# Score products of a linear-attention branch issued as pairs of 64x64 products on two column tiles, and moved behind the weight tiles

## The chip, the cores and the metric

The kernel runs on one core of one Trainium2 chip. The metric is the device time of one execution in microseconds (us), and the number that counts is the median of several runs. TensorE (PE) does the matrix products, VectorE (DVE) and ScalarE (ACT) do elementwise work, GpSimd (POOL) prepares weights, SyncE (SP) issues the weight transfers. All five run their own instruction streams and wait for each other by semaphores.

## The reference, cut to what matters

The network is a trunk of two layers at 512 tokens and width 1024. The even layer mixes an HGRN2 branch (8 heads of 128) with an RWKV-7 branch (16 heads of 64). The change touches the scores of the HGRN2 branch, here for one head and one chunk:

```
G = jnp.cumsum(gc, axis=2)
diff = jnp.where(causal[:, :, None], G[:, :, :, None, :] - G[:, :, None, :, :], -jnp.inf)
attn = jnp.einsum('bhtk,bhsk,bhtsk->bhts', qc, kc, jnp.exp(diff))
o = jnp.einsum('bhts,bhsv->bhtv', attn, vc) + jnp.einsum('bhtk,bhkv->bhtv', qc * jnp.exp(G), state)
```

So `attn[t, s]` is a dot product over the 128 channels in which every channel is damped by the decay between s and t. The RWKV-7 branch is a recurrence over chunks of a state per head; its hops from chunk to chunk ("the chain" below) are what the score products are interleaved with.

## The kernel before

The even layer runs in nine rounds, `even_round(i)`, i = 0 to 8. Round i projects the input for head i (tiles 0 to 7, each `t(j)` made of two halves of 12 products of 512 columns, whose weights come in two units) and computes HGRN2 for head i, while RWKV-7 is computed for the pair of heads of round i - 1. Round 0 has no RWKV-7 part, round 8 has nothing else; rounds 1 to 7 have both, and rounds 2 to 7 are a hardware loop. The odd layer and the output projections follow and are not touched.

HGRN2 takes chunks of 128 tokens (CH = 4, L = 128) and builds the damping up in seven levels: level `lvl` covers the pairs of blocks of m = 2^lvl tokens, the later block being the queries and the earlier one the keys. VectorE and ScalarE rescale queries and keys from level to level (`level` L1375 on VectorE, `level_copies` L903 on ScalarE), TensorE multiplies them (`hg_level`, one 128x128 product per chunk into bank 2 or 3 of PSUM), and VectorE copies the pairs that belong to the level into `attn` with a mask (`masked`, L1398, by a predicated copy at L1361). Level 6 needs one 64x64 block per chunk alone and is already issued so. The diagonal (`hg_diagonal`) is an eighth set of products. Levels 0 to 5 and the diagonal have nonzero pairs only inside the two 64x64 blocks on the diagonal of a chunk.

The chain of RWKV-7 has three steps of TensorE per chunk: `chain_rhs` (rhs), `chain_u` (u) and `chain_out` (out). Between rhs and u, ScalarE copies the result out of PSUM (`chain`, L969), between u and out again, and between out of one chunk and rhs of the next VectorE updates the state (`state`, L1502; for chunks 1 and 2 these are the lines L1513 and L1516). TensorE's own order is written out by hand; its waits are in order, and so are those of every other engine. In VectorE's order, `state(r, 1)` stands behind the masked copies of levels 0 and 1, and `state(r, 2)` stands behind the masked copy of level 2, the rescaling of level 5 (L1394 to L1396) and the masked copy of level 3.

GpSimd splits every weight unit in two (L255 and L257) as soon as TensorE has finished the unit that held the same of four slots; `half_tile` waits for the split unit and, in its first half, for its PSUM bank.

Of the kernel before, what the change touches and what calls it, by code (L numbers as in the profile page):

```python
# [21 lines left out]
P = 128  # L22
KC = D // P
CH = 4
L = T // CH
# [62 lines left out]
def count(name, r, j=0):  # L88

    value = r * PER_ROUND[name] + j + 1  # L90
    assert not isinstance(value, int) or value > 0, (name, r, j)
    return value


def trunk(nc, xT, pT, wall, par_e, par_o, gains, w2a2, lru_w, masks, out):
    ctx = ExitStack()
    with ctx:
# [32 lines left out]
        psum = ctx.enter_context(nc.psum_tensor("psum", [P, 8, T], F32))  # L130
        bank = [psum[:, n, :] for n in range(8)]
        H0, H1, R0, R1, R2, R3 = bank[2:8]
# [15 lines left out]
        hq, hk, hf, hv, sig_a, sig_b, g_a = (place(T) for _ in range(7))  # L148
        qp = place(4 * T).rearrange("p (r t) -> p r t", r=4)
# [120 lines left out]
        def _(pe):  # L270
            def mm(o, lhsT, rhs, start=True, stop=True):
                return pe.matmul(o, lhsT, rhs, start=start, stop=stop, skip_group_check=True)  # L272
# [186 lines left out]
            def chain_u(r, c):  # L459

                pe.wait_ge(sem["rw_rhse"], count("rw_rhse", r, c))
                for e, rows in heads:
                    last = mm(R0[:, 64 + 64 * e:128 + 64 * e], inv[:, c, 2 + e, :], rhs_s[:, c % 2, rows])
                last.then_inc(sem["rw_u"], 1)
# [38 lines left out]
            def hg_level(r, lvl):  # L503

                o = bank[2 + lvl % 2]
                pe.wait_ge(sem["hg_lvl"], count("hg_lvl", r, lvl))
                if lvl:
                    pe.wait_ge(sem["hg_even"], count("hg_even", r, 2 * lvl - 1))
                if lvl == 0:
                    pe.wait_ge(sem["hg_vtok"], count("hg_vtok", r))  # L510
                elif lvl == 1:
                    if not (isinstance(r, int) and r == 0):
                        pe.wait_ge(sem["hg_n"], count("hg_n", r - 1))
                else:
                    pe.wait_ge(sem["hg_masked"], count("hg_masked", r, lvl - 2))
                keys = hk if lvl == 0 else kr[:, lvl % 4, :]
                for c in range(CH):
                    at = slice(c * L, (c + 1) * L)
                    if lvl < LEVELS - 1:
                        last = mm(o[:, at], keys[:, at], qp[:, lvl % 4, at])  # L520
                    else:
                        even, odd = slice(c * L, c * L + 64), slice(c * L + 64, (c + 1) * L)
                        last = mm(o[0:64, odd], keys[:, even], qp[:, lvl % 4, odd])
                last.then_inc(sem["hg_qk"], 1)

            def hg_diagonal(r):
                pe.wait_ge(sem["hg_masked"], count("hg_masked", r, 5))
                for c in range(CH):
                    last = mm(H1[:, c * L:(c + 1) * L], hk[:, c * L:(c + 1) * L], hq[:, c * L:(c + 1) * L])
                last.then_inc(sem["hg_qk"], 1)  # L530

            def hg_keys(r):
# [32 lines left out]
            def even_round(i, head=True, pair=True):  # L565

                r = i - 1
                first = isinstance(i, int) and i == 0

                def t(j, halves=(0, 1)):  # L570
                    if head or j == 0:
                        for half in halves:
                            half_tile(i, j, half, 0, "free", first and j < 2, 0 if first and j == 0 else None)

                def level(lvl):
                    if head:
                        hg_level(i, lvl)

                def embedding(m):
                    if not head:  # L580
                        if m == 0:
                            pe.wait_ge(sem["free0"], count("free0", EV_ROUNDS, 0))
                            pe.wait_ge(sem["free1"], count("free1", EV_ROUNDS - 1, 3))
                        else:
                            pe.wait_ge(sem["prj_evac"], count("prj_evac", 0, m - 1))
                        embed(0, m, U_PRJ0, (0, 1))

                t(0)
                if pair:
                    low_rank(r)  # L590
                t(1)
                if pair:
                    key_norm(r)
                    bonus(r)
                embedding(0)
                t(2)
                t(3)
                if pair:
                    transposes(r)
                    t(4, (0,))  # L600
                    for n in range(2 * CH):
                        product(r, n)
                        if n >= 3 and n % 2:
                            inverse_start(r, n // 2 - 1)
                    t(4, (1,))
                    inverse_start(r, 3)
                    for lvl in range(1, 7):
                        inverse(r, lvl)
                    chain_rhs(r, 0)
                    t(5, (0,))  # L610
                    chain_u(r, 0)
                    t(5, (1,))
                    chain_out(r, 0)
                else:
                    t(4)
                    t(5)
                embedding(1)
                if head:
                    hg_values(i)
                if pair:  # L620
                    chain_rhs(r, 1)
                level(0)
                if pair:
                    chain_u(r, 1)
                level(1)
                if pair:
                    chain_out(r, 1)
                embedding(2)
                t(6)
                if pair:  # L630
                    chain_rhs(r, 2)
                level(2)
                if pair:
                    chain_u(r, 2)
                level(3)
                if pair:
                    chain_out(r, 2)
                embedding(3)
                t(7)
                if pair:  # L640
                    chain_rhs(r, 3)
                level(4)
                if pair:
                    chain_u(r, 3)
                level(5)
                if pair:
                    chain_out(r, 3)
                level(6)
                if head:
                    hg_diagonal(i)  # L650
                    hg_keys(i)
                if pair:
                    head_mean(r)
                if head:
                    hg_changes(i)
                    hg_outputs(i)
                if pair:
                    head_var(r)
                if head:
                    hg_norm(i)  # L660
# [602 lines left out]
        def _(dve):  # L1263
# [48 lines left out]
                    ins.then_inc(sem["bias_set"], 1)  # L1312

            dve.memset(attn, 0.0)
            dve.memset(p_full, 0.0)
            dve.memset(shift[:, 0:1], 0.0)
            dve.memset(w2_slot[64:P, 0, :], 0.0)
# [589 lines left out]
```

## Time and profile before

| | us |
|---|---|
| median of 3 runs (range) | 1501.81 (1501.2 to 1503.7) |
| span of the profiled execution | 1501.0 |
| TensorE busy | 1391.1 |
| VectorE busy | 792.6 |
| ScalarE busy | 560.3 |
| GpSimd busy | 622.7 |

The profiled span runs from the first to the last instruction of the program and is 0.8 us under the median of the runs. An engine's busy time counts instructions in progress; waits, register and branch instructions do not count. TensorE's products overlap, and each product of 32-bit operands shows two entries (its two passes), each product of 512 columns with split operands shows one.

### The profile page before, as it was taken

How to read it: one execution, taken by the hardware profiler on the slowest of the kernel's cores; microseconds unless marked ns; L12 is line 12 of the kernel's file. 1: busy time of each engine (PE TensorE's matmuls, PEld its weight loads, DVE VectorE, ACT ScalarE, POOL GpSimd, SP SyncE). 2: the span in 40 equal slices, each digit the busy share in tenths (PEclk: the TensorE clock that was granted, in tenths of full speed). 3: DMA queues.
4: the chain of work that ended last, by engine and by line, in shares of the span. 5: the costliest groups of instructions: out<-in, count | busy, mean ns of one | idle time of the engine just before them, and what ended most of it. 6: DMA issues, size and time to landing. Idle time of an engine off the chain costs nothing. (4 is left out here: it accounts for less than half of the span.)

```text
span 1501.0 us, 24358 instructions
## 1 busy us (share of the span) xinstructions
PE 1391.1 (93%) x7722; PEld 1109.9 (74%) x7722; DVE 792.6 (53%) x1412; ACT 560.3 (37%) x1214; POOL 622.7 (41%) x584
## 2 busy tenths in 40 slices
PE   2999999999999999999999979899979999998995
PEld 1776877877878877868868857787757777776874
DVE  6546256365275374373373462207674747566457
ACT  3333344344244254244344353203242433335123
POOL 3643133242241350350251201577844636454872
PEclk9999999999999999999999989999979999999998
DMA  5211011011110120120120100333312212221331
GB/s 177 80 52 49 21 53 43 29 45 41 28 58 28 42 57 14 42 65 7 42 65 14 41 30 16 125 108 91 98 56 71 78 56 77 67 66 50 103 93 63
DMA packets 46687, 87.80 MB, mean 58 GB/s; under 512 B 5808, under 2 KB 6832, under 8 KB 46384
## 3 DMA queue, kind: packets, MB, share of 16 engines
q1 hardware_dynamic: 44352, 82.44, 18.5%
q10 hardware_dynamic: 2288, 4.72, 0.9%
q8 instruction: 31, 0.51, 0.1%
q14 instruction: 16, 0.13, 0.0%
HBM read 85.04 MB, written 2.10 MB: 58 GB/s over the span
## 5 line engine op out<-in xcount | busy, mean ns | idle before, releaser
L272 PE MATMUL psum<-h_split,w_hi 128*128 128x512 f32 x2320 | 754.5, 407 | 17.0 <-DVE h_split L1275 9.0
L255 POOL TENSOR_SCALAR w_hi<-w_raw 128x512 fp32r<-128x512 f32 x290 | 213.2, 735 | 828.1 <-PE psum L272 705.8
L272 PEld LDWEIGHTS psum<-h_split,w_hi 128*128 128x128 f32 x2320 | 438.9, 192 | 134.2 <-issue 37.8
L272 PE MATMUL psum<-mix 128*128 128x128 f32 (+4 forms) x3520 | 485.4, 292 | 19.2 <-ACT mix L831 7.0
L272 PE MATMUL psum<-h_split,w_lo 128*128 128x512 f32 x1160 | 458.8, 396 | 0.0
L272 PEld LDWEIGHTS psum<-mix 128*128 128x128 f32 (+1 forms) x3520 | 379.4, 176 | 89.5 <-issue 45.8
L257 POOL TENSOR_TENSOR w_lo<-w_raw,w_hi 128x512 fp32r<-128x512 f32 x290 | 410.5, 1416 | 24.2
L831 ACT ACTIVATE mix<-psum 128x256 f32<-128x256 f32 (+5 forms) x624 | 233.1, 391 | 459.8 <-PE psum L272 251.0
L272 PEld LDWEIGHTS psum<-h_split,w_lo 128*128 128x128 f32 x1160 | 222.1, 191 | 48.6
L1361 DVE COPY_PREDICATED mix<-mask,psum 128x128 f32<-128x128 uint8 (+2 forms) x312 | 135.6, 465 | 187.3 <-PE psum L272 184.3
L831 ACT ACTIVATE mix<-mix 128x512 f32<-128x512 f32 (+3 forms) x274 | 137.9, 538 | 158.9 <-DVE mix L1636 72.4
L831 ACT ACTIVATE mix<-psum,mix 128x512 f32<-128x512 f32 (+2 forms) x88 | 53.4, 631 | 170.1 <-PE psum L272 122.0
L272 PE MATMUL psum<-mix,fconst 128*128 128x512 f32 x90 | 51.1, 666 | 49.5 <-DVE mix L1295 38.7
L1271 DVE SCALAR_TENSOR_TENSOR mix<-psum,mix 128x512 f32<-128x512 f32 x40 | 29.5, 736 | 113.1 <-ACT mix L831 101.7
L1271 DVE SCALAR_TENSOR_TENSOR mix<-mix 128x512 f32<-128x512 f32 (+1 forms) x72 | 75.8, 1053 | 12.8 <-ACT mix L831 10.5
L272 PEld LDWEIGHTS psum<-mix,fconst 128*128 128x128 f32 x90 | 14.9, 200 | 65.1 <-issue 21.4
L419 PE MATMUL psum<-fconst,mix 128*128 128x128 f32 x320 | 62.1, 276 | 0.1
L1361 DVE COPY_PREDICATED psum<-mask,fconst 128x128 f32<-128x128 uint8 x32 | 14.6, 455 | 58.2 <-PE psum L272 58.2
L831 ACT ACT_TABLE_LOAD x23 | 29.5, 1283 | 41.5 <-PE psum L272 37.0
L1306 DVE TENSOR_TENSOR h_split<-y,h_split 128x512 fp32r<-128x512 f32 x28 | 25.2, 941 | 37.0 <-ACT h_split L831 37.0
L419 PEld LDWEIGHTS psum<-fconst,mix 128*128 128x128 f32 x320 | 39.3, 142 | 1.4 <-DVE mix L1361 0.3
L1275 DVE TENSOR_TENSOR h_split<-mix,h_split 128x512 fp32r<-128x512 f32 x32 | 34.7, 1085 | 10.7 <-ACT h_split L831 10.4
(118 smaller groups left out, 733.3 us busy)
## 6 DMA issues: line engine op xcount, KB each, us to landing
w_raw<-wall SPq DMA_DIRECT2D x290, 256.0 KB, 2.6
mix<-xT SPq DMA_DIRECT2D x4, 512.0 KB, 6.3
mix<-xT ACTq DMA_DIRECT2D x1, 2048.0 KB, 8.0
out<-mix SPq DMA_DIRECT2D x8, 256.0 KB, 2.1
mix<-mask_f SPq DMA_DIRECT2D x1, 1792.0 KB, 11.4
mix<-pT ACTq DMA_DIRECT2D x2, 512.0 KB, 3.5
mix<-lru_w ACTq DMA_DIRECT2D x4, 256.0 KB, 3.3
mix<-w2a ACTq DMA_DIRECT2D x16, 32.0 KB, 2.8
```

Of the source, the lines that this page charges most:

```text
L255: pool.tensor_scalar(w_hi[:, slot, :, :], w_raw[:, slot, :], 1.0, 0.0, ALU.mult, ALU.add).then_inc(sem["w_hi"], 1)
L257: pool.tensor_tensor(w_lo[:, slot, :, :], w_raw[:, slot, :], w_hi[:, slot, :, :].bitcast(F32).rearrange("p k n -> p (k n)"), ALU.subtract) ...
L272: return pe.matmul(o, lhsT, rhs, start=start, stop=stop, skip_group_check=True)
L419: last = pe.transpose(bank[2 + c % 2][:, e * P:(e + 1) * P], inv[:, c, e, :], ident)
L831: return act.activation(o, i, func, bias=bias, scale=scale, **kw)
L1271: return dve.scalar_tensor_tensor(out=o, in0=a, scalar=scalar, in1=b, op0=op0, op1=op1)
L1275: dve.tensor_tensor(h_split[:, KC + c, :], hn[:, c % 2, :], h_split[:, c, :].bitcast(F32), ALU.subtract).then_inc(sem["h_ready"], 1)
L1306: dve.tensor_tensor(h_split[:, KC + ring, :], y[:, rows[c], :], h_split[:, ring, :].bitcast(F32), ALU.subtract).then_inc(sem["y_split"], 1)
L1361: return dve.copy_predicated(dst, mask, src)
```

## The change

Each of the products of levels 0 to 5 and of the diagonal, 128x128 per chunk, becomes two 64x64 products per chunk: the even half of a chunk writes partitions 0 to 63 of PSUM (one column tile of the array, 64 columns wide), the odd half partitions 64 to 127 (the other column tile). The off-diagonal blocks of the two banks are not written any more, so they are set to zero once at the start. In TensorE's order, the tiles 6 and 7 move ahead: one half of tile 6 now stands between rhs and u of chunk 1 and one half behind u, and the levels 0 and 1 follow together, right ahead of out of chunk 1; the same is done with tile 7, chunk 2 and the levels 2 and 3. The levels 4 to 6, the diagonal and all orders of VectorE, ScalarE and GpSimd stay as they are, but for the one memset.

```
                 for c in range(CH):
-                    at = slice(c * L, (c + 1) * L)
+                    even, odd = slice(c * L, c * L + 64), slice(c * L + 64, (c + 1) * L)
                     if lvl < LEVELS - 1:
-                        last = mm(o[:, at], keys[:, at], qp[:, lvl % 4, at])
+                        mm(o[0:64, even], keys[:, even], qp[:, lvl % 4, even])
+                        last = mm(o[64:P, odd], keys[:, odd], qp[:, lvl % 4, odd])
                     else:
-                        even, odd = slice(c * L, c * L + 64), slice(c * L + 64, (c + 1) * L)
                         last = mm(o[0:64, odd], keys[:, even], qp[:, lvl % 4, odd])
...
                 for c in range(CH):
-                    last = mm(H1[:, c * L:(c + 1) * L], hk[:, c * L:(c + 1) * L], hq[:, c * L:(c + 1) * L])
+                    even, odd = slice(c * L, c * L + 64), slice(c * L + 64, (c + 1) * L)
+                    mm(H1[0:64, even], hk[:, even], hq[:, even])
+                    last = mm(H1[64:P, odd], hk[:, odd], hq[:, odd])
...
                 if pair:
                     chain_rhs(r, 1)
+                t(6, (0,))
+                if pair:
+                    chain_u(r, 1)
+                t(6, (1,))
                 level(0)
-                if pair:
-                    chain_u(r, 1)
                 level(1)
                 if pair:
                     chain_out(r, 1)
                 embedding(2)
-                t(6)
                 if pair:
                     chain_rhs(r, 2)
+                t(7, (0,))
+                if pair:
+                    chain_u(r, 2)
+                t(7, (1,))
                 level(2)
-                if pair:
-                    chain_u(r, 2)
                 level(3)
                 if pair:
                     chain_out(r, 2)
                 embedding(3)
-                t(7)
                 if pair:
                     chain_rhs(r, 3)
...
             dve.memset(attn, 0.0)
+            dve.memset(psum[:, 2:4, :], 0.0)
```

In the loop of rounds 2 to 7, TensorE's order from out of chunk 2 to level 4 was as follows. All products have the helper's line L272; a shape of 128x64 waiting for rw_s and rw_ue is rhs, one waiting for rw_rhse is u, the 64x64 and 64x128 ones are out, those that wait for hg_masked and hg_even are levels, and the ones with h_split are tile 7, of which the first rows stand here.

```order
L272 MATMUL psum<-mix 64x64 [waits rw_s,rw_ue]
L272 MATMUL psum<-mix 64x64 x3
L272 MATMUL psum<-mix 64x128 x6
L286 REGISTER_ALU [waits free1]
L272 MATMUL psum<-h_split,w_hi 128x512 [waits w_ready]
L272 MATMUL psum<-h_split,w_hi 128x512
L272 MATMUL psum<-h_split,w_lo 128x512
```

Tile 7 stood between out of chunk 2 and rhs of chunk 3, behind the levels 2 and 3. The changed kernel has, from the end of tile 7 to level 4:

```order
L506 REGISTER_ALU
L508 REGISTER_ALU [waits hg_lvl]
L272 MATMUL psum<-mix 64x64 [waits hg_masked,hg_even]
L272 MATMUL psum<-mix 64x64 x7
L506 REGISTER_ALU
L508 REGISTER_ALU [waits hg_lvl]
L272 MATMUL psum<-mix 64x64 [waits hg_masked,hg_even]
L272 MATMUL psum<-mix 64x64 x7
L272 MATMUL psum<-mix 64x64 [waits rw_s,rw_ue]
L272 MATMUL psum<-mix 64x64 x3
L272 MATMUL psum<-mix 64x128 x6
L272 MATMUL psum<-mix 128x64 [waits rw_s,rw_ue]
```

The levels 2 and 3 now come after tile 7, as eight 64x64 products each, and rhs of chunk 3 (last row) follows out of chunk 2 directly.

On VectorE nothing of the loop moves. Its rows from the masked copy of level 2 (first row) to the state update of chunk 2 (last two rows) are, in both kernels:

```order
L1361 COPY_PREDICATED mix<-mask,psum 128x64x4 [waits hg_qk,hg_masked]
L1385 REGISTER_ALU
L1387 REGISTER_ALU [waits hg_lvl]
L1394 TENSOR_TENSOR mix<-mix 128x16x16 [waits hg_qk,hg_even]
L1395 TENSOR_TENSOR mix<-mix 128x16x16
L1396 TENSOR_TENSOR mix<-mix 128x16
L1361 COPY_PREDICATED mix<-mask,psum 128x32x8 [waits hg_qk,hg_masked]
L1512 REGISTER_ALU [waits rw_s,rw_st]
L1513 TENSOR_TENSOR mix<-psum,mix 128x64 [waits rw_yc]
L1516 TENSOR_SCALAR mix<-mix 128x64 [waits rw_sadd]
```

What moved is what the first of them waits for: the level 2 products now end after tile 7, not before it.

## Rows read from the trace of the kernel before

**Rows 1.** Busy time (count) of PE, PEld, DVE, ACT, POOL; clock; DMA: one round

```profile
208.30:316.40 108.10, 105.49 (x678) 86.16 (x677) 55.35 (x113) 44.80 (x108) 34.32 (x32) 1.00 0.13 41
```

**Rows 2.** Timeline (start, duration, what, entries) of TensorE: tile 5's halves, u, out

```profile
817.02 0.71 PE L272 MATMUL psum<-h_split,w_hi 128*128 128x512 f32 x2
...
819.88 0.56 PE L272 MATMUL psum<-mix 128*128 128x64 f32 x4
820.25 0.71 PE L272 MATMUL psum<-h_split,w_hi 128*128 128x512 f32 x2
...
823.15 0.46 PE L272 MATMUL psum<-mix 128*64 128x64 f32 x8
```

**Rows 3.** TensorE, short stretches of chunk 1: rhs, level 0, out, tile 6

```profile
824.51 1.00 PE L272 MATMUL psum<-mix 128*128 128x64 f32 x8
...
825.37 1.16 PE L272 MATMUL psum<-mix 128*128 128x128 f32 x8
...
827.79 0.46 PE L272 MATMUL psum<-mix 128*64 128x64 f32 x8
...
828.08 1.09 PE L272 MATMUL psum<-mix 128*64 128x128 f32 x12
829.10 0.50 PE L272 MATMUL psum<-h_split,w_hi 128*128 128x512 f32 x1
```

**Rows 4.** TensorE, end of round 7: rhs of chunk 3, out, hg_keys

```profile
844.79 1.00 PE L272 MATMUL psum<-mix 128*128 128x64 f32 x8
...
848.00 0.93 PE L272 MATMUL psum<-mix 128*64 128x128 f32 x10
...
850.44 0.33 PE L537 MATMUL psum<-fconst,mix 128*128 128x128 f32 x1
```

**Rows 5.** Timeline of GpSimd, round 7, second operation of two weight splits

```profile
824.12 1.31 POOL L257 TENSOR_TENSOR w_lo<-w_raw,w_hi 128x512 fp32r<-128x512 f32 x1
...
845.84 1.27 POOL L257 TENSOR_TENSOR w_lo<-w_raw,w_hi 128x512 fp32r<-128x512 f32 x1
```

**Rows 6.** Timeline of VectorE, round 7: masked copies, state updates, rescaling

```profile
828.04 0.73 DVE L1361 COPY_PREDICATED mix<-mask,psum 128x256 f32<-128x256 uint8 x1 [0.64 <-PE psum L272]
...
828.85 0.25 DVE L1516 TENSOR_SCALAR mix<-mix 128x64 f32<-128x64 f32 x1
829.11 0.43 DVE L1394 TENSOR_TENSOR mix<-mix 128x256 f32<-128x256 f32 x1
...
838.13 0.44 DVE L1361 COPY_PREDICATED mix<-mask,psum 128x256 f32<-128x256 uint8 x1 [0.15 <-PE psum L272]
...
838.75 0.25 DVE L1516 TENSOR_SCALAR mix<-mix 128x64 f32<-128x64 f32 x1
...
846.46 0.94 DVE L1394 TENSOR_TENSOR mix<-mix 128x256 f32<-128x256 f32 x1
...
847.73 1.00 DVE L1361 COPY_PREDICATED mix<-mask,psum 128x256 f32<-128x256 uint8 x2
```

**Rows 7.** Timeline of ScalarE, round 7: rhs copy, then level 7 copies

```profile
825.55 0.28 ACT L831 ACTIVATE mix<-psum 128x128 f32<-128x128 f32 x1 [0.24 <-PE psum L272]
...
849.68 0.71 ACT L831 ACTIVATE mix<-mix 128x256 f32<-128x256 f32 x2
```

**Rows 8.** Timeline of TensorE, round 0: levels 0 and 1, then hg_keys

```profile
69.62 2.52 PE L272 MATMUL psum<-mix 128*128 128x128 f32 x16 [1.94 <-ACT mix L831]
...
90.95 0.52 PE L537 MATMUL psum<-fconst,mix 128*128 128x128 f32 x3
```

**Rows 9.** Timeline of VectorE, round 0: last projection copy, rescaling, masked level 6

```profile
86.74 0.75 DVE L1271 SCALAR_TENSOR_TENSOR mix<-psum,mix 128x512 f32<-128x512 f32 x1 [4.77 <-ACT mix L831]
87.41 1.02 DVE L1394 TENSOR_TENSOR mix<-mix 128x256 f32<-128x256 f32 x1
...
90.40 0.41 DVE L1403 COPY mix<-psum 64x256 f32<-64x256 f32 x1
```

**Rows 10.** Timeline of VectorE at the start

```profile
12.39 1.88 DVE L1295 TENSOR_TENSOR mix<-mix 128x512 f32<-128x512 f32 x2 [4.54 <-DMA mix<-xT]
```

More of the change, by code:

```diff
@@ L621, in even_round @@
                     chain_rhs(r, 1)
-                level(0)
+                t(6, (0,))
                 if pair:
                     chain_u(r, 1)
+                t(6, (1,))
+                level(0)
                 level(1)
@@ L628, in even_round @@
                 embedding(2)
-                t(6)
                 if pair:
                     chain_rhs(r, 2)
-                level(2)
+                t(7, (0,))
                 if pair:
                     chain_u(r, 2)
+                t(7, (1,))
+                level(2)
                 level(3)
```

## The prediction, made blind

> **What bounds the kernel now.** I read the busy time by stretch first. A repeated round of the even layer lasts 108.10 us and TensorE works in 105.49 us of it, at full clock (2.4 GHz) [rows 1]; the seven rounds 1 to 7 look alike. VectorE and ScalarE are at half load or less. So TensorE's own queue bounds these rounds, with small gaps, and the reader is to see two questions: how much work leaves the queue, and whether a wait opens that the long tiles 6 and 7 used to cover.
>
> Then I read round 7 instruction by instruction on TensorE. From rhs of chunk 1 (824.51) to rhs of chunk 3 (844.79) it takes 20.28 us, and from there to hg_keys (850.44) 5.65 us [rows 3, 4]. In the first stretch lie tiles 6 and 7 and the levels 0 to 3.
>
> **What a level costs, wide and narrow.** From rhs to out of chunk 1 there are 3.28 us [rows 3]: rhs 0.86 us, one hop u 0.37 us (819.88 to 820.25) [rows 2], so two wide levels take 2.05 us, 1.03 each with the changes of width. The trace has no narrow level, but it has the same form: the state part of out, four 64x64 products that use both column tiles, issues its 8 entries in 0.28 us (827.79 to 828.08) [rows 3]. That is two tiles side by side: 0.07 us per product. Twice that is 0.56 us for a level; the first entries after a change of width are the slow ones, so I take 0.5, and 1.0 for two levels in a row. The bound on the other side is that a long run does not overlap like a short one. Then the cost stays near that of a wide level, 0.9 us, and nothing is gained per level. I take the low end, since the row is of the same shape and both tiles.
>
> The page TensorE: Matmul & The Clock Gate of the Trainium skill (Part 3, What overlaps and what doesn't) speaks against the change: a weight load overlaps with products in flight only if it goes to other rows of the array. Both column tiles use all rows, so by that rule their loads would not overlap, and the sum would be near that of rival (b) below. The 8 entries in 0.28 us, loads included, contradict it, so I follow the row.
>
> **Stretch 1, rhs 1 to rhs 2.** TensorE: rhs 0.85, half of tile 6 2.86 (817.02 to 819.88), u 0.37, other half with the change to narrow 2.90 (820.25 to 823.15) [rows 2], together 6.98 us to the first product of level 0; call this moment L. Two levels 1.0, out 1.31 (827.79 to 829.10) [rows 3]: TensorE is ready for rhs 2 at L + 2.3. But rhs 2 waits for `state(r, 1)` on VectorE, which stands behind the masked copies of levels 0 and 1. Before, tile 6 stood there and covered it. VectorE: level 0 ends at L + 0.7, the copy starts 0.17 later (0.15 idle beside a row that waited for the same) at L + 0.86 and takes 0.73; the next follows at L + 1.63; from its start to that of L1516 are 0.81 us (828.04 to 828.85), L1516 takes 0.25 [rows 6]: the state is there at L + 2.69. TensorE starts 0.14 after an end on VectorE (90.40 + 0.41 to 90.95) [rows 8, 9]: L + 2.83. New wait 0.5 us; the stretch is 9.81 us.
>
> **Stretch 2, rhs 2 to rhs 3.** Again 6.98 us to L, and ready at L + 2.3. Behind level 2, VectorE has more to do before `state(r, 2)`: masked copy, the three rescalings of level 5, masked copy. Here GpSimd comes in. Its second operation of a split starts 0.97 us after the first narrow product behind a half tile (823.15 to 824.12) [rows 2, 5] and takes 1.3 us, so it holds L + 0.97 to L + 2.28. L1394 would start at L + 1.2 to 1.3, right in it. In the trace L1394 takes 0.43 us alone, but 0.94 us when it begins (846.46) inside that operation of GpSimd (845.84 to 847.11); it ends 0.29 us after it [rows 5, 6]. This repeats in every round at level 6. So L1394 ends at L + 2.54 instead of L + 1.7; the copy of level 3 starts 0.33 later (847.40 to 847.73), L1516 0.62 after that (838.13 to 838.75), it takes 0.25 [rows 6], and TensorE is released 0.14 later: L + 3.88. New wait 1.6 us; the stretch is 10.86 us.
>
> The page SBUF — State Buffer of the Trainium skill (section SBUF: two separate sides) gives the rule: a VectorE operation with two SBUF inputs and a GpSimd operation exclude each other, and who comes first holds the port for the whole instruction. The rows agree: only such operations wait for GpSimd here, while copies from PSUM do not. The rule has a second side: if L1394 begins before L + 0.97, it holds the port and GpSimd waits, which is rival (a) below and its 1491.7 us; my times put it 0.25 us behind.
>
> Sum of the two stretches: 20.67 us against 20.28 us before. The four narrow levels save some 2.1 us, the half tiles cost 0.4 more for two more changes of shape, and the two waits eat 2.1. So +0.4 us.
>
> **Stretch 3, rhs 3 to hg_keys, 5.65 us before.** Rhs to out was 3.21 us (844.79 to 848.00) [rows 4]. The levels 4 and 5 save 0.3 each: level 4 is a visit to the narrow mode and back, and each change shows some 0.1 to 0.15 us. That gives 2.6; u has ended at 2.2, ScalarE's copy (0.28) [rows 7] and the release put out at about 2.75. From out to hg_keys it took 2.44 us (848.00 to 850.44), and that is not TensorE's work: hg_keys waits for the level 7 copies of ScalarE, which end at 850.39 [rows 4, 7] and stand behind its copy of the outputs of the chain. So the narrower diagonal saves nothing. Stretch 3 becomes 5.2 us: -0.5. What follows (states, outputs, norm) hangs on hg_keys as before.
>
> Net per round: +0.4 - 0.5 = -0.1 us. Seven rounds: -0.8 us.
>
> **Round 0** has no chain. Before, TensorE waited 1.94 us for ScalarE ahead of level 0 (from 67.68) [rows 8]; now tile 6 (5.7 us, two halves of 2.86) fills this. Level 0 starts at 67.6 + 5.7 = 73.3, tile 7 at 74.4, level 2 at L = 80.1. L1394 is held as above until L + 2.5, the rescaling of level 5 is through at 83.0, ScalarE does its two copies (0.71) [rows 7] and a copy of tile 7 of about the same length, so VectorE gets to its last projection copy at 84.45, which was at 86.74 [rows 9]. From there to hg_keys were 4.21 us (to 90.95) [rows 8], of which 0.6 us were L1394 held by GpSimd (1.02 instead of 0.43) [rows 6, 9]; GpSimd will be done by then. So hg_keys comes at 88.1 instead of 90.95: -2.9 us.
>
> **The start.** The memset of two PSUM banks (1024 columns) delays VectorE by about 1 us. It then idles 4.54 us for the input to land [rows 10]: no cost; without that cover 1 us.
>
> **Sum:** -0.8 - 2.9 = -3.7 us on the profiled execution (span 1501.0, which is 0.8 under the median): 1501.8 - 3.7 = 1498.1 us.
>
> **The rivals.**
> (a) VectorE is not held in stretch 2, because L1394 begins before GpSimd's operation, or the split comes later. For it: 0.25 us decide. Against: it needs both the products and the copy faster than any row. The wait shrinks by 0.9 us per round: 1498.1 - 6.4 = 1491.7 us. Chance 0.15.
> (b) Slower: the two column tiles do not run side by side in long runs, so a narrow level costs 0.9 instead of 0.5. Stretch 1 gains 0.4 (its wait takes up the rest), stretch 2 nothing (1.6 us of wait are there already), stretch 3 0.9: +1.3 per round, and about 1 us in round 0: 1498.1 + 9 + 1 = 1508 us. It decides from about 0.2 us more per level. For it: no row shows more than a few products in this form. Against: the 8 entries in 0.28 us. Chance 0.10.
> (c) Small waits that I cannot see: each level is preceded by register and wait instructions on TensorE's queue that the wide products covered, and narrow ones cover less; a release may take 0.3 instead of 0.14 us. At 0.5 us per round the gain of the rounds is gone: 1501.6, no change. Chance 0.15.
> (d) The clock: TensorE idles 2 us more per round, and in round 0 it sits in waits between levels 4 and 6. If it falls to 1.2 GHz after them, a wide product takes twice as long for a while; 1 us per round gives 1505. Against: at full clock a round already holds some 2.6 us without work on TensorE [rows 1]. Chance 0.05.
>
> **How the numbers follow.** My forecast has 0.55, with its own range 1495 to 1501.5 (0.4 us per round either way). About 0.2% (3 us) is what a measurement of this kernel can tell from no change. The bound is 1498.8, so a bit over 6 in 10 of my forecast lies in faster: 0.35 and 0.15 from (a) is 0.50. Same gets the rest, 0.20, most of (c), and a sliver of (d): 0.34. Slower: (b), most of (d), a tail of (c): 0.16. The range that leaves out 2 in 10 goes from (a) to just short of (d): 1491.5 to 1504.5.
>
> **What the changed profile would show.** Narrow levels as 16 entries in about 0.5 us. TensorE idle ahead of rhs 2 by 0.5 and ahead of rhs 3 by 1.6 us, put down to L1516. L1394 behind the copy of level 2 at about 1.3 us instead of 0.43, ending 0.29 us after GpSimd's operation, in each of the seven rounds. A round of about 108.0 us; hg_keys of round 0 at 88. I am wrong if L1394 takes 0.43 us there, if 16 entries take 0.9 us, or if the clock of the rounds is under 1.00.

## The result, and the profile after

The changed kernel takes 1507.7 us (median; 1505.9 to 1509.0) against 1501.8 us (1501.2 to 1503.7) for the kernel before in the same comparison: a ratio of 1.0038, 95% interval 1.0025 to 1.0050. It is slower by 0.4%, about 6 us, where 1498.1 was forecast and the range ended at 1504.5. The profiled execution has a span of 1505.7 us, against 1501.0 before.

First, busy time by stretch of the changed kernel. The first seven rows are the rounds 1 to 7, from one hg_keys to the next; the last is a piece of round 2. Columns as in [rows 1].

```profile
86.16:199.31 113.15, 105.23 (x729) 85.76 (x730) 52.26 (x109) 43.02 (x104) 32.00 (x32) 0.96 0.13 39
199.31:308.87 109.56, 104.20 (x734) 84.42 (x734) 55.65 (x113) 44.63 (x107) 34.31 (x32) 0.98 0.15 40
308.87:418.39 109.52, 104.17 (x734) 84.36 (x734) 55.82 (x113) 44.61 (x107) 33.99 (x32) 0.98 0.15 39
418.39:528.62 110.23, 105.43 (x734) 85.51 (x734) 55.42 (x112) 44.60 (x107) 33.96 (x32) 0.97 0.14 39
528.62:636.86 108.24, 102.88 (x733) 83.18 (x734) 56.09 (x113) 44.60 (x107) 33.97 (x32) 1.00 0.13 39
636.86:746.36 109.50, 104.15 (x733) 84.33 (x733) 55.86 (x113) 44.60 (x107) 33.98 (x32) 0.98 0.14 39
746.36:854.42 108.06, 102.70 (x733) 82.90 (x734) 55.54 (x113) 44.61 (x107) 34.52 (x32) 1.00 0.13 39
303.90:307.30 3.40, 3.40 (x35) 3.28 (x36) 1.90 (x7) 0.28 (x1) 0.00 (x0) 0.50 0.02 5
```

Read the granted clock (third column from the right) beside the length. The two rounds at 1.00 take 108.24 and 108.06 us, as forecast (108.0). The other four of the rounds 2 to 7 are at 0.97 or 0.98 and take 1.3 to 2.2 us more. In each of them the clock stands at 0.50 (1.2 GHz) for one piece, as in the last row. The mean granted clock of all five runs is 0.969 to 0.972; that of the kernel before, in its runs beside the later kernels, is 0.976 to 0.982.

Where the piece lies shows against one row of the kernel before, over its rounds 2 to 7:

```profile
201.83:850.44 648.61, 633.05 (x4062) 517.02 (x4062) 332.87 (x672) 268.86 (x642) 204.38 (x192) 1.00 0.14 40
```

and two rows of the changed kernel, each from the first product of rhs 3 to hg_keys, in round 2 (with a piece at half clock) and in round 7 (without):

```profile
302.19:308.87 6.68, 6.05 (x81) 5.67 (x81) 3.85 (x11) 2.33 (x6) 0.00 (x0) 0.74 0.10 36
849.31:854.42 5.11, 4.47 (x80) 4.13 (x81) 3.73 (x11) 2.32 (x6) 0.00 (x0) 1.00 0.07 24
```

The same work (80 or 81 entries, two to a product) takes 1.57 us longer in round 2. What the engine did just before is in the timeline of TensorE, here of round 7 (start, duration, what, entries, idle time and its releaser):

```profile
835.52 2.31 PE L272 MATMUL psum<-mix 128*64 128x64 f32 x52
838.46 1.08 PE L272 MATMUL psum<-mix 128*128 128x64 f32 x8 [0.62 <-DVE mix L1521]
...
845.47 2.31 PE L272 MATMUL psum<-mix 128*64 128x64 f32 x52
849.31 4.48 PE L272 MATMUL psum<-mix 128*128 128x64 f32 x80 [1.52 <-DVE mix L1521]
854.42 0.55 PE L539 MATMUL psum<-fconst,mix 128*128 128x128 f32 x3 [0.64 <-ACT mix L835]
```

These are the two new waits, 0.62 us ahead of rhs 2 and 1.52 us ahead of rhs 3, put down to `state` (L1516 before, now L1521). The 52 entries are two narrow levels (32) and out (20): 2.31 us, where the two wide levels (2.05) and out up to the end of its last product (827.79 to 829.17, 1.38, in [rows 3]) took 3.4. The waits repeat in all seven rounds; so says the view of TensorE's waits (total, times, longest):

```profile
PE psum L272 <- DVE mix L1521: 15.1, 14, 1.5
```

The second wait on the side of VectorE and GpSimd, round 7; L1399 is L1394 of the kernel before:

```profile
846.35 0.45 DVE L1366 COPY_PREDICATED mix<-mask,psum 128x256 f32<-128x256 uint8 x1 [6.51 <-PE psum L272]
846.69 1.29 DVE L1399 TENSOR_TENSOR mix<-mix 128x256 f32<-128x256 f32 x1
...
848.90 0.25 DVE L1521 TENSOR_SCALAR mix<-mix 128x64 f32<-128x64 f32 x1
```

```profile
846.43 1.27 POOL L257 TENSOR_TENSOR w_lo<-w_raw,w_hi 128x512 fp32r<-128x512 f32 x1
```

L1399 takes 1.29 us instead of the 0.43 of [rows 6] and ends at 847.98, 0.28 us after GpSimd's operation (847.70). The local mechanism is the one that was forecast.

In the sum of the profiled executions, hg_keys of round 0 comes 4.8 us earlier (86.16 against 90.95), round 1 is 2.3 us longer (113.15 against 110.88), the rounds 2 to 7 are 6.5 us longer (655.1 against 648.6), and what follows is 0.7 us longer: +4.7 us. Of the 4.8 us, 1.6 lie ahead of everything that the change moved; the product that stands ahead of level 0 starts that much earlier (first row before, second row changed):

```profile
67.08 0.60 PE L500 MATMUL psum<-fconst,mix 128*128 128x128 f32 x4
```

```profile
65.49 0.60 PE L500 MATMUL psum<-fconst,mix 128*128 128x128 f32 x4
```

The 2.3 us of round 1 lie at its very start. Between hg_keys of round 0 and the first product with split weights behind it there are 4.93 us before (first row) and 7.34 us in the changed kernel (second row), at a clock of 0.58:

```profile
90.95:95.88 4.93, 3.66 (x28) 2.99 (x26) 1.71 (x4) 1.09 (x2) 0.00 (x0) 1.00 0.00 0
```

```profile
86.16:93.50 7.34, 6.07 (x26) 5.14 (x26) 1.70 (x4) 1.09 (x2) 0.00 (x0) 0.58 0.01 2
85.50:92.30 6.80, 5.83 (x31) 4.97 (x27) 2.23 (x7) 0.51 (x2) 0.00 (x0) 0.50 0.01 2
```

The last row is the piece at half clock. Ahead of it TensorE waited twice for ScalarE, ahead of level 5 and of level 6:

```profile
81.67 0.69 PE L272 MATMUL psum<-mix 128*64 128x64 f32 x16 [1.28 <-ACT mix L835]
84.54 1.28 PE L272 MATMUL psum<-mix 128*64 128x64 f32 x24 [2.19 <-ACT mix L835]
```

So the question for the runs was whether the half clock comes from the waits or from the narrow products themselves.

### The profile page after: what moved, and what is told of

Same layout as the page of the kernel before. It is cut to its first block, busy times and chain, and to the rows that moved or that the text cites. A ratio compares the mean times of both kernels' runs of the same rounds, so it can differ in the third digit from the quotient of the medians.

```text
span 1505.7 us, 25255 instructions
## 1 busy us (share of the span) xinstructions
PE 1376.8 (91%) x8170; PEld 1092.4 (73%) x8170; DVE 793.7 (53%) x1413; ACT 558.5 (37%) x1214; POOL 623.6 (41%) x584
## 4 chain that ended last, share of the span: by engine, by line
PE 70%; DVE 14%; issue 5%; ACT 4%; DVEq 0%; ACTq 0%
PE psum L272 65%; ACT mix L835 3%; PE psum L419 2%; DVE mix L1275 2%; DVE mix L1366 1%; DVE mix L1299 1%; PE psum L773 1%; DVE mix L1476 1%; DVE mix L1474 1%; DVE mix L1742 1%; DVE mix L1658 1%; ACT L1013 1%; DVE mix L1669 1%; PE psum L348 1%; DVE mix L1475 1%
## 5 line engine op out<-in xcount | busy, mean ns | idle before, releaser
L272 PE MATMUL psum<-h_split,w_hi 128*128 128x512 f32 x2320 | 754.1, 407 | 17.4 <-DVE h_split L1279 9.4
L272 PEld LDWEIGHTS psum<-h_split,w_hi 128*128 128x128 f32 x2320 | 437.2, 192 | 131.5 <-issue 36.1
L272 PE MATMUL psum<-mix 128*128 128x128 f32 (+4 forms) x3968 | 474.0, 283 | 34.6 <-DVE mix L1521 15.1
L272 PE MATMUL psum<-h_split,w_lo 128*128 128x512 f32 x1160 | 458.7, 395 | 0.0
L272 PEld LDWEIGHTS psum<-mix 128*128 128x128 f32 (+1 forms) x3968 | 365.7, 170 | 112.4 <-issue 67.8
L257 POOL TENSOR_TENSOR w_lo<-w_raw,w_hi 128x512 fp32r<-128x512 f32 x290 | 411.9, 1420 | 24.2
L272 PEld LDWEIGHTS psum<-h_split,w_lo 128*128 128x128 f32 x1160 | 221.4, 191 | 48.1
L272 PE MATMUL psum<-mix,fconst 128*128 128x512 f32 x90 | 50.8, 663 | 48.9 <-DVE mix L1299 37.8
L272 PEld LDWEIGHTS psum<-mix,fconst 128*128 128x128 f32 x90 | 15.0, 200 | 64.3 <-issue 20.6
```

The lines of the kernel that those rows point to most:

```text
L257: pool.tensor_tensor(w_lo[:, slot, :, :], w_raw[:, slot, :], w_hi[:, slot, :, :].bitcast(F32).rearrange("p k n -> p (k n)"), ALU.subtract) ...
```

## The experiments

**Narrow products, old order.** The order of TensorE is that of the kernel before:

```
-                t(6, (0,))
+                level(0)
                 if pair:
                     chain_u(r, 1)
-                t(6, (1,))
-                level(0)
                 level(1)
                 if pair:
                     chain_out(r, 1)
                 embedding(2)
+                t(6)
```

and the same for tile 7 and the levels 2 and 3.

> Narrow products alone: the 64x64 pairs of the change in the order of before. Theory W (what costs is the new wait ahead of rhs 3 and the fall of TensorE's clock that follows it): no new wait exists here, each of the three stretches from rhs to out gets 0.5 us shorter, a repeated round takes 106.6 us at full clock instead of 108.10, round 0 gives 2 us: about 1489 us. Rival N (narrow products by themselves let the clock fall): the same savings, but falls of the clock in most rounds, 1.4 us each: about 1499 us.

Measured: 1490.4 us (1488.0 to 1492.7), ratio 0.9926 [0.9909, 0.9943]. Rounds 2 to 7, by stretch:

```profile
195.86:833.46 637.60, 619.43 (x4398) 503.01 (x4399) 333.11 (x673) 268.59 (x642) 204.15 (x192) 1.00 0.14 40
```

A round takes 106.27 us at full clock. The narrow products alone are 11.4 us faster than before, and do not let the clock fall in these rounds. The loss comes in with the order.

**Wide products, new order.** The products are those of before, and the order is that of the change:

```
-                        mm(o[0:64, even], keys[:, even], qp[:, lvl % 4, even])
-                        last = mm(o[64:P, odd], keys[:, odd], qp[:, lvl % 4, odd])
+                        last = mm(o[:, at], keys[:, at], qp[:, lvl % 4, at])
```

> The move alone: wide products in the new order. Theory W: the wait ahead of rhs 3 shrinks from 1.5 to 0.7 us, because two wide levels fill more of it, but the levels cost 0.5 us more each: a round takes 109.0 us at full clock, round 0 gives 3 to 4 us: 1504 us without falls of the clock, and some falls where the wait is still long enough. Rival N: wide products keep the clock up, every round at clock 1.00: 1504 us. If falls are as frequent as in the changed kernel, 1511 us.

Measured: 1506.6 us (1504.1 to 1509.9), ratio 1.0031 [1.0020, 1.0042]. The waits ahead of rhs 3:

```profile
PE psum L272 <- DVE mix L1518: 4.7, 7, 0.7
```

The six rounds take 653.78 us (109.0 each) with a granted clock of 1.00. With a wait of 0.7 us instead of 1.5 the clock stays up, and the order costs 0.9 us per round by its waits and changes of shape. The median is 2.6 us over the expected 1504; the rounds were as expected, and round 1, which took 114.02 us with a piece at half clock at its start like the changed kernel's, was not in that sum.

**Work in the wait.** The changed kernel, with one product whose result nobody reads ahead of rhs 3, in the rounds that have a chain:

```
+            def filler(r):
+                pe.wait_ge(sem["free0"], count("free0", r + 1, 3))
+                mm(bank[0][:, :], ones, hk)
...
                 embedding(3)
+                if pair and head:
+                    filler(r)
                 if pair:
                     chain_rhs(r, 3)
```

> The changed kernel with one more product per repeated round, 512 columns of 32-bit operands (0.86 us) into a free PSUM bank, right ahead of the wait of rhs 3; nobody reads it. Theory W: the wait of 1.5 us covers it, the array is busy in most of it, and the falls of the clock go: each round 108.1 us at clock 1.00, about 1501 us, faster than the changed kernel by 6 us although it does more. Rival N: the falls stay, 1507.7 us. If the extra product does not fit under the wait, 1507.7 + 6 = 1514 us.

Measured: 1501.3 us (1497.8 to 1503.6), ratio 0.9995 [0.9985, 1.0005]. Timeline of TensorE in round 7 (the first row is the new product), and the rounds 2 to 7 by stretch:

```profile
843.67 1.13 PE L272 MATMUL psum<-mix,fconst 128*128 128x512 f32 x2
845.26 4.48 PE L272 MATMUL psum<-mix 128*128 128x64 f32 x80 [0.46 <-DVE mix L1528]
```

```profile
202.47:850.38 647.91, 622.07 (x4411) 499.39 (x4411) 333.96 (x673) 267.67 (x642) 204.12 (x192) 1.00 0.14 40
```

The wait is 0.46 us now. Rhs 3 comes no earlier (10.84 us behind rhs 2, against 10.85), no work has left the queue, one product more is done in each of the rounds 1 to 7, and the kernel is 6.4 us faster than the changed one. The six rounds take 647.9 instead of 655.1 us. So the idle time ahead of rhs 3 costs twice: itself, and the clock behind it. The second cost is shown here, since the product changes nothing but what TensorE does in that time.

**Tile 6 alone, tile 7 alone.** Narrow products; in the first kernel tile 7 and the levels 2 and 3 are put back, in the second tile 6 and the levels 0 and 1, as in the diff above.

> Narrow products; tile 6 is moved between the hops of chunk 1 as in the change, tile 7 and the levels 2 and 3 stay as in the kernel before. From rhs 1 to rhs 2 TensorE took 9.48 us with narrow products in the old order and 9.87 us in the changed kernel (new wait 0.62 us). So a round takes 106.27 + 0.39 = 106.66 us. Theory W (the clock falls only behind the wait of 1.5 us ahead of rhs 3): no fall of the clock in the rounds, median 1490.4 + 7 x 0.39 = 1493. Rival S (a wait of 0.6 us behind a run of narrow products is enough): falls of the clock in some rounds, 1.4 us each, 1497 to 1500.

Measured: 1489.8 us (1488.3 to 1492.0), ratio 0.9928 [0.9911, 0.9944].

```profile
196.99:837.50 640.51, 618.54 (x4399) 501.05 (x4399) 332.42 (x673) 268.59 (x642) 204.49 (x192) 1.00 0.14 40
```

Rounds of 106.75 us (106.66 expected), clock 1.00. The median is 3 us under the expected one: in the profiled execution the six rounds are 2.9 us longer than with the old order, and the stretch behind hg_keys of round 7 is 3.2 us shorter (649.4 against 652.6). The layers behind vary by that much between executions of kernels that do not differ there, and this limits what a median can tell.

> Narrow products; tile 7 and the levels 2 and 3 are moved as in the change, tile 6 and the levels 0 and 1 stay as in the kernel before. From rhs 2 to rhs 3 it was 9.48 us with narrow products in the old order and 10.85 us in the changed kernel (wait 1.52 us), so an undisturbed round takes 106.27 + 1.37 = 107.64 us, and seven of them give 1490.4 + 9.6 = 1500. Theory W (this wait alone makes the clock fall): granted clock of 0.50 behind the wait ahead of rhs 3 in about half of the rounds, 1.4 us or more each, median about 1505 to 1507. Rival B (both waits of a round are needed): no falls, 1500.

Measured: 1509.4 us (1501.8 to 1513.3, 12 runs), ratio 1.0046 [1.0029, 1.0063]. The rounds 2 to 7, and one piece:

```profile
201.79:853.55 651.76, 624.55 (x4398) 506.72 (x4399) 334.71 (x673) 267.96 (x642) 204.23 (x192) 0.99 0.14 39
306.50:309.90 3.40, 3.40 (x48) 3.40 (x49) 1.56 (x6) 0.87 (x3) 0.00 (x0) 0.51 0.02 5
```

Two rounds take 107.6 and 107.8 us, as expected (107.64), and four hold a piece at half clock behind rhs 3 and take 108.8 to 109.7. The median is 2.4 us above the upper end of what was expected. The profiled run is one of the shorter ones (1506.8 us, mean clock 0.970); the longest have mean clocks down to 0.965, so they lost more to the clock than the profile shows. The wait of 0.6 us was followed by no fall, that of 1.5 us by falls without the other. Rival S and rival B fall.

**A long wait behind wide products.** Is it the narrow products ahead of the wait as well? The wide kernel in the new order, with two copies on VectorE that delay `state(r, 2)`:

```
+                    if lvl == 3:
+                        dve.tensor_copy(spare[:, 0:512], bank[3][:, :])
+                        dve.tensor_copy(spare[:, 512:640], bank[3][:, 0:128])
                     masked_copy(dst, mask, src).then_inc(sem["hg_masked"], 1)
```

> Wide products in the new order (as in the kernel that took 1506.6 us, whose wait ahead of rhs 3 was 0.67 us), and VectorE copies 640 columns of a bank of PSUM into unused SBUF ahead of its masked copy of level 3, 0.95 us more work, so that TensorE waits 1.6 us ahead of rhs 3, as long as in the changed kernel (1.52). A round takes 108.97 + 0.95 = 109.9 us. Theory L (the length of the wait alone decides): the clock falls in some rounds, 1.4 us each, median 1513 + 5 to 6 = 1519. Theory C (the wait and the narrow products ahead of it together): no falls, median 1506.6 + 6.6 = 1513.

Measured: 1515.6 us (1511.0 to 1518.7), ratio 1.0090 [1.0069, 1.0111]: between the two theories. The waits ahead of rhs 3, the rounds 2 to 7 and one of the pieces:

```profile
PE psum L273 <- DVE mix L1522: 10.3, 7, 1.5
```

```profile
200.01:861.63 661.62, 636.61 (x4062) 519.69 (x4062) 337.76 (x684) 267.68 (x642) 204.18 (x192) 0.99 0.13 39
305.80:309.20 3.40, 3.40 (x17) 3.18 (x16) 0.64 (x2) 0.28 (x1) 0.00 (x0) 0.50 0.00 0
```

Four rounds take 109.7 us and two, with such a piece, 111.4 and 111.3. So narrow products are not needed: a wait of 1.5 us behind wide ones was followed by the same piece at half clock. In this execution it was two rounds of six, with narrow products four of six. One profile each does not settle whether that difference is real; the mean clocks of all runs (0.973 to 0.979 here, 0.969 to 0.972 for the changed kernel) point the same way.

**State updates first.** If the wait is the trouble, VectorE's order should change with TensorE's. Of the changed kernel: `state(r, 1)` ahead of the masked copy of level 1, `state(r, 2)` ahead of the rescaling of level 5, VectorE's mixing of tile 7 behind the masked copy of level 5, ScalarE's chunk 3 ahead of its copies of level 6 and of the shifted tile 7:

```
                     masked(i, 0)
-                    masked(i, 1)
                 if pair:
                     state(r, 1)
+                if head:
+                    masked(i, 1)
...
                     masked(i, 2)
-                    level(i, 5)
-                    masked(i, 3)
                 if pair:
                     state(r, 2)
+                if head:
+                    level(i, 5)
+                    masked(i, 3)
```

> The changed kernel with other orders on VectorE and ScalarE: the state updates of chunks 1 and 2 go ahead of the masked copy of level 1 and ahead of the rescaling of level 5 that GpSimd holds up; ScalarE serves the chain of chunk 3 before the copies of level 6 and tile 7. Theory W: the waits ahead of rhs 2 (0.6) and rhs 3 (1.5) go, and with them the falls of the clock: rounds of 106.0 us, about 1485 us; 1487 if hg_keys comes 0.2 us later for the later copies. Rival N: the waits go but falls of the clock stay, 1492 us.

Measured: 1490.4 us (1484.8 to 1492.5), ratio 0.9913 [0.9895, 0.9931]. The rounds take 106.8 us, not 106.0 to 106.2, at full clock. The waits for `state` are gone, and TensorE's waits have a new row:

```profile
PE psum L539 <- DVE mix L1409: 10.5, 8, 1.4
```

hg_keys (L539) now waits 1.4 us for VectorE's masked copy of level 6. What was saved went there: VectorE mixed tile 7 late, and that stood ahead of this copy. In the rounds 1 to 7 this wait of up to 1.4 us was followed by no fall of the clock.

**And hg_keys released early.** Of the kernel with the state updates first: VectorE mixes tile 7 right behind the masked copy of level 3; ScalarE copies the shifted tile 7 ahead of the chain's chunk 3 and makes the level 7 copies ahead of the chain's outputs.

```
                     masked(i, 3)
+                    mixed(i, 2, 7, wv)
...
                     masked(i, 5)
-                    mixed(i, 2, 7, wv)
                     level(i, 7)
```

> The kernel with the state updates first, in which hg_keys waited up to 1.4 us for VectorE's masked copy of level 6. Now ScalarE copies the shifted tile 7 ahead of the chain's chunk 3, VectorE mixes tile 7 behind the masked copy of level 3 and not behind that of level 5, and ScalarE makes its level 7 copies ahead of the copy of the chain's outputs. VectorE's masked copy of level 6 then ends some 1.1 us earlier (its 0.35 us of idle time and 0.75 us of mixing lie in a gap where it waited for products), so a round takes 106.81 - 1.0 = 105.8 us and the median is 1490.4 - 7 = 1483.5. Rival: the release of hg_keys passes to ScalarE, whose level 7 copies end where they ended, and nothing changes: 1490.

Measured: 1482.2 us (1481.0 to 1485.1), ratio 0.9877 [0.9859, 0.9895]. The rounds take 105.73 us (105.8 expected). Round 1 still took 112.7 us, with a piece of 13.7 us at half clock that begins at the end of round 0.

**Work in the waits of round 0.** Of the kernel just described, with the same filling product behind level 4 and behind level 5 in round 0 alone, and in a second kernel also behind hg_keys:

```
                 level(4)
+                if first:
+                    filler(i)
                 if pair:
                     chain_u(r, 3)
                 level(5)
+                if first:
+                    filler(i)
```

> The fastest version so far (1482.2 us), with two products of 512 columns of 32-bit operands, 0.86 us each, whose result nobody reads, in round 0 alone: behind level 4 and behind level 5. There TensorE waited 1.27 and 1.05 us for ScalarE, and from 81.8 on it ran at a granted clock of 0.50 for 13.7 us, in which 9.4 us of work are entered. Both fit into the waits, so no level comes later. Theory W (a wait lets the clock fall, also here): no fall at 81.8 or one much shorter, and round 1 takes 108.5 instead of 112.74 (105.7 + the 2.8 that round 1 had over a repeated round in the kernel before), median 1478. Rival: the clock falls anyway behind the later waits ahead of the state changes and outputs (0.58 and 0.69), median 1481 to 1482.

> As the one with two filling products in round 0, with a third one behind hg_keys in round 0, in the wait of 0.58 us for ScalarE's copy; it is longer than the wait by 0.3 us. Theory W: where the two already keep the clock up, this costs 0.3 us in one round and gives nothing that can be measured: 1478 to 1479. If two leave a fall behind hg_keys, the third takes it away: 1478 against 1481 for two.

Measured: 1477.7 us (1477.0 to 1479.9, 4 runs) with two, ratio 0.9856 [0.9839, 0.9872], and 1478.6 us (1477.6 to 1479.1), 0.9862 [0.9845, 0.9878], with three. These two ran on another chip, where the kernel before took 1499.1 us, so the ratios compare better than the medians; against 0.9877 the intervals overlap, and the traces, one profile each, have to decide. By stretch, the end of round 0 and its outputs, then round 1, first without and then with two fillers:

```profile
84.50:98.00 13.50, 12.23 (x43) 9.56 (x43) 3.37 (x8) 3.69 (x5) 0.62 (x1) 0.59 0.01 1
...
84.52:197.26 112.74, 107.16 (x730) 87.04 (x730) 51.47 (x109) 43.02 (x104) 31.99 (x32) 0.94 0.14 39
```

```profile
84.50:98.00 13.50, 12.23 (x59) 9.17 (x58) 4.89 (x13) 5.67 (x8) 3.83 (x4) 1.00 0.08 21
...
84.32:191.10 106.78, 101.20 (x730) 82.33 (x730) 51.45 (x109) 43.09 (x104) 32.09 (x32) 1.00 0.15 41
```

In the same 13.5 us TensorE goes through 59 entries instead of 43, at a clock of 1.00 instead of 0.59, and round 1 is 6.0 us shorter, 1.7 us more than expected (108.5). The third product changes nothing: round 1 takes 106.78 us again.

Not all of the 6.0 us is explained by the filled waits. Up to the products that stand at 99.71 in the one and at 95.13 in the other, 4.4 us are gained; the other 1.6 us come from a second piece at half clock, at 122.8, that is gone too. The waits ahead of that one are not filled, and are the same without fillers (first two rows) and with them (last two):

```profile
121.22 0.63 PE L348 MATMUL psum<-fconst,mix 128*128 128x128 f32 x4 [1.50 <-DVE mix L1476]
122.80 1.97 PE L348 MATMUL psum<-fconst,mix 128*128 128x128 f32 x8 [0.95 <-DVE mix L1477]
```

```profile
116.64 0.63 PE L348 MATMUL psum<-fconst,mix 128*128 128x128 f32 x4 [1.50 <-DVE mix L1485]
118.22 1.09 PE L348 MATMUL psum<-fconst,mix 128*128 128x128 f32 x8 [0.95 <-DVE mix L1486]
```

All twelve profiled kernels have these two waits (1.50 and 0.95 or 0.96 us). In ten a piece at half clock follows, in the two with fillers in round 0 none does. So a wait of 1.5 us does not fix by itself whether the clock falls.

This is the fastest version that was run, 1.4% under the kernel before.

## Why the prediction was wrong

The step that failed is rival (d), the clock. I gave it 0.05 and put no term for it into the forecast, on the ground that "at full clock a round already holds some 2.6 us without work on TensorE" [rows 1]. That sum counts idle time over a whole round; it says nothing of one wait of 1.5 us in one piece, and that is what my own working had put ahead of rhs 3. The runs show the cost: 6.2 us in the rounds 2 to 7 (655.1 against six rounds of 108.15), gone with the filling product, absent with tile 6 alone, there with tile 7 alone and with wide products and an equal wait. And 2.4 us more at the start of round 1, behind the waits between levels 4 and 6 of round 0 that (d) names too. The size given for (d), "1 us per round", was about right; the chance was wrong.

The trace of the kernel before already held the warning. The wait of 1.94 us ahead of level 0 in [rows 8] and the two in round 1 below are each followed by a piece at half clock (last two rows):

```profile
123.27 0.63 PE L348 MATMUL psum<-fconst,mix 128*128 128x128 f32 x4 [1.50 <-DVE mix L1470]
124.85 1.30 PE L348 MATMUL psum<-fconst,mix 128*128 128x128 f32 x8 [0.95 <-DVE mix L1471]
```

```profile
71.00:74.40 3.40, 3.40 (x12) 2.91 (x12) 2.04 (x5) 0.59 (x2) 0.00 (x0) 0.50 0.18 60
125.60:129.00 3.40, 3.40 (x12) 2.72 (x10) 0.81 (x2) 3.17 (x5) 0.00 (x0) 0.50 0.21 76
```

The prediction says that the seven rounds 1 to 7 look alike; round 1 is the one of 110.88 us with such a piece.

In the profiled executions -3.7 us were forecast and +4.7 came. Of the difference of 8.4 us, about 6.2 are the clock in the rounds 2 to 7, 2.4 the clock at the start of round 1, 0.9 undisturbed rounds of 108.15 us instead of 108.0, and 0.7 lie behind the last round; round 0 gave 1.9 us more than forecast. That the median lies at rival (b)'s 1508 is a coincidence: (b) needs a narrow level of 0.9 us, and it took 0.5.

Step by step:

- **A narrow level in 0.5 us**: right. The 52 entries take 2.31 us; out's first product starts 0.98 us behind level 2's first (845.47 to 846.45), so two levels are 0.98 us, 0.52 and 0.47. For these products the page TensorE: Matmul & The Clock Gate of the Trainium skill (Part 3, What overlaps and what doesn't) would have a weight load overlap only with products on other rows. The trace disagrees in the long run too, as it did in the 8 entries of [rows 3]: their weight loads, 0.13 to 0.14 us each, all start within these 0.98 us, beside products in flight.
- **Wait of 0.5 us ahead of rhs 2**: 0.62. **Wait of 1.6 us ahead of rhs 3**: 1.52. **Both stretches, 20.67 us**: 828.59 to 849.31, 20.72. The port rule of the page SBUF — State Buffer of the Trainium skill (section SBUF: two separate sides) agrees: held at 846.69, ended 0.28 us after GpSimd's operation. The prediction's reading that only operations with two SBUF inputs wait was too narrow: in the kernel before, L1566, with one such input, takes 1.51 to 1.52 us in the repeated rounds beside GpSimd's L257, and 0.47 us in round 1, with nothing of GpSimd beside it.
- **Rhs 3 to hg_keys, 5.2 us**: 5.11 in round 7. hg_keys did wait for ScalarE (0.64 us), so the narrow diagonal saved nothing, as said.
- **A round of 108.0**: 108.06 and 108.24 in the two rounds at full clock. Without the falls the rounds would have come out as forecast.
- **Round 0, -2.9 us**: -4.8 at hg_keys, of which 1.6 were there before level 0 and owe nothing to the moved tiles; from L500 to hg_keys it is 20.67 us against 23.87, so -3.2, close to the forecast. In part this is luck: the kernel before had 3.4 us at half clock in this stretch, which the working did not price. Round 1 gave 2.3 us back. In the version with the waits of round 0 filled, round 1 is 1.1 us longer than a repeated round; before the change it was 2.8 longer, after it 5.0 (113.15 against 108.15). That the added part is clock is read in the trace of the changed kernel (0.58 in the stretch of 7.34 us); that filling the waits takes it away was run on the later version only.
- **The memset**: 0.91 us, and VectorE still idles 2.75 us for the input behind it: no cost, as said.

The large loss against what the narrow products can give has a second part. In the old order they save 1.83 us per round (106.27 against 108.10), in the new one only 0.8 (108.15 against 108.97), since rhs 2 and rhs 3 wait for VectorE, and rhs 3 through it for GpSimd, whose time does not depend on them: the wait ahead of rhs 3 grows from 0.67 to 1.52 us, and that of 0.62 us ahead of rhs 2, which the wide products do not have, is new. Over six rounds the lost saving is some 6 us, as large as the clock's part. The narrow products in the old order were never costed by themselves in the prediction: I took the change as a whole against before and saw -0.1 us per round, without asking what each half was worth.

What stays open: which rounds are hit (four of six in the profiled execution; the 12 runs of the kernel with tile 7 alone spread over 11.6 us), why a wait of 1.4 us ahead of hg_keys was not followed by a fall, and why the waits of 1.50 and 0.95 us in round 1 were followed by one in ten kernels and not in the two with fillers in round 0.

## What to carry to other kernels

Price a new wait on TensorE twice: for its length, and for the work behind it at half clock, if the wait is in one piece; the mean idle share of a round says nothing on that, but a look at the granted clock behind the waits that the kernel already has does. Before a shorter product is put beside a reordering, work out each alone: here the one gave 11.4 us and the other took 4.7, and together they lost 5.9 (each against the kernel before, beside which it ran). Where another engine's operation releases the wait, move that operation ahead of work that nobody waits for, then look at who is late next; where the wait can't be removed, a product that nobody reads can cost less than nothing.

## What the runs showed of the hardware

- A wait of 1.5 us ahead of rhs 3 was followed by a granted clock of 0.50 for 3.4 or 6.8 us in four of the six rounds 2 to 7 (two of six with wide products), at 1.1 to 2.2 us each; waits of 0.5 to 0.7 us ahead of rhs 2 or 3 by none in 18 rounds (wide products in the new order, the filling product, tile 6 alone, six rounds each). The wait alone does not decide: 1.4 us ahead of hg_keys was followed by no fall in seven rounds, and 1.50 and 0.95 us in round 1 by one in ten of twelve kernels.
- A product that does nothing useful (1.13 us in the timeline) made the kernel 6.4 us faster; with two of them in round 0, round 1 was 6.0 us shorter, 4.4 of it right behind them.
- Pairs of 64x64 products on two column tiles keep their pace in long runs: two levels, 32 entries, take 0.98 us, against 2.05 us for the 16 entries of two 128x128 levels.
- An elementwise operation of VectorE on SBUF that meets a running operation of GpSimd ends behind it: L1399 1.29 us instead of 0.43, ended 0.28 us behind GpSimd's end; the copy out of PSUM at 846.35 beside the same operation took its usual 0.45 us.
